# Two norm passes of a transformer kernel rearranged: who adds x, in what order the K tiles come, and from where the high parts are taken

## The reference, cut to what matters

```python
hx = rmsnorm(x, g_pre1) * (1.0 + sc1) + sh1            # the norm in front (pre1)
ux = hx @ w_in                                         # q, k, v, pooling, convolution, gates
yx = mixer_out(...)                                    # attention, pooling, convolution, merged @ w_out
x  = x + gt1 * rmsnorm(yx, g_post1)                    # the norm behind (post1), added to x
hx2 = rmsnorm(x, g_pre2) * (1.0 + sc2) + sh2           # pre2
x  = x + gt2 * rmsnorm(swiglu(hx2, w_ffn_in, w_ffn_out), g_post2)      # post2
```

## Time and profile before

| | before |
|---|---|
| median of three runs | 2203.57 us (2198.2 to 2205.74) |
| the profiled execution | 2197.6 us; the span of its instructions is 2195.8 us |
| PE busy | 2114.2 us, 96% of the span |
| DVE / ACT / POOL busy | 1335.3 / 799.6 / 772.2 us (61%, 36%, 35%) |
| mean granted clock of PE | 0.986 of full speed |

### The profile page before, as it was taken

The page is one execution under the profiler, slowest core; times in us unless marked ns, Lnnn a source line. Parts: engine busy times, 40 slices in busy tenths (PEclk is TensorE's granted clock), DMA queues, the critical chain, the costliest instruction groups (busy, mean ns, idle before and its releaser), DMA issues.

```text
span 2195.8 us, 27998 instructions
## 1 busy us (share of the span) xinstructions
PE 2114.2 (96%) x11316; PEld 1783.8 (81%) x11316; DVE 1335.3 (61%) x1807; ACT 799.6 (36%) x1173; POOL 772.2 (35%) x360
## 2 busy tenths in 40 slices
PE   8989999999999999999999989899999999999997
PEld 7777888888888888888888877778777877888885
DVE  8379899755873788757517775989854262101113
ACT  5457412234234522222212345662244343222223
POOL 3310123232335434233323345004344465444442
PEclk9999999999999999999999989999999999999998
DMA  7100011132452233533323322002222422222321
GB/s 273 58 30 1 25 58 63 48 107 92 144 193 86 74 125 122 197 104 116 107 84 114 96 75 83 26 1 82 86 93 85 141 78 96 93 91 95 96 87 67
DMA packets 63200, 202.62 MB, mean 92 GB/s; under 512 B 7136, under 2 KB 8416, under 8 KB 63072
## 3 DMA queue, kind: packets, MB, share of 16 engines
q1 hardware_dynamic: 58608, 191.56, 26.3%
q10 hardware_dynamic: 4464, 9.28, 1.2%
HBM read 195.17 MB, written 5.64 MB: 91 GB/s over the span
## 4 chain that ended last, share of the span: by engine, by line
PE 78%; DVE 18%; ACT 2%; issue 1%; DMA 0%; POOL 0%; ACTq 0%; DVEq 0%; POOLq 0%
PE ps L545 73%; DVE conv_acc L1719 3%; DVE unit_stats L1680 2%; DVE ps L1719 2%; DVE probs L1694 1%; DVE pt1l L1700 1%; DVE pt0l L1700 1%; PE ps L677 1%; PE ps L571 1%; PE ps L804 1%; DVE ada_raw L1550 1%; PE ps L647 1%; PE ps L825 1%; PE ps L656 1%; DVE acc L1441 1%
## 5 line engine op out<-in xcount | busy, mean ns | idle before, releaser
L445 POOL TENSOR_TENSOR w_l<-w_raw,w_h 128x1024 fp32r<-128x1024 f32 (+3 forms) x296 | 673.8, 2281 | 1285.5 <-ACT w_h L961 1285.2
L545 PE MATMUL ps<-h_h,w_h 128*128 128x512 f32 (+1 forms) x1296 | 428.6, 371 | 9.2 <-ACT t L1241 4.2
L545 PE MATMUL ps<-h_h,w_l 128*128 128x512 f32 (+1 forms) x1296 | 425.1, 368 | 0.0
L545 PE MATMUL ps<-h_l,w_h 128*128 128x512 f32 (+1 forms) x1296 | 425.1, 368 | 0.0
L961 ACT ACTIVATE w_h<-w_raw 128x1024 fp32r<-128x1024 f32 (+3 forms) x296 | 277.2, 938 | 222.3 <-PE ps L545 148.6
L545 PEld LDWEIGHTS ps<-h_h,w_h 128*128 128x128 f32 x1296 | 244.2, 189 | 59.3 <-ACT t L1241 6.6
L545 PEld LDWEIGHTS ps<-h_h,w_l 128*128 128x128 f32 x1296 | 244.9, 189 | 43.3
L545 PEld LDWEIGHTS ps<-h_l,w_h 128*128 128x128 f32 x1296 | 244.5, 189 | 42.4 <-issue 1.2
L1550 DVE CUSTOM_DVE_ANT_0 ps<-ada_raw,c_row 128x1024 f32<-128x1024 f32 x160 | 272.3, 1702 | 9.0 <-DMA ada_raw<-in_ada 4.0
L545 PE MATMUL ps<-f_h,w_h 128*128 128x258 f32 (+1 forms) x672 | 173.1, 339 | 0.9 <-DVE t L1905 0.9
L545 PE MATMUL ps<-f_h,w_l 128*128 128x258 f32 (+1 forms) x672 | 173.5, 340 | 0.0
(11 more groups left out here) (266 smaller groups left out, 3189.1 us busy)
## 6 DMA issues: line engine op xcount, KB each, us to landing
w_raw<-in_w SPq DMA_DIRECT2D x216, 512.0 KB, 3.6
ada_raw<-in_ada SPq DMA_DIRECT2D x80, 512.0 KB, 3.6
w_raw<-in_w SPq DMA_DIRECT2D x56, 256.0 KB, 3.0
w_raw<-in_w SPq DMA_DIRECT2D x16, 384.0 KB, 3.0
ada_near<-in_ada SPq DMA_DIRECT2D x10, 512.0 KB, 10.0
ada_far<-in_ada SPq DMA_DIRECT2D x6, 512.0 KB, 14.8
x_again<-in_x ACTq DMA_DIRECT2D x8, 384.0 KB, 7.3
x_between<-x SPq DMA_DIRECT2D x8, 384.0 KB, 2.3
```

Of the source, the lines that this page charges most:

```text
L445: nc.gpsimd.tensor_tensor(wl[:, s % RING, 0:n], raw[:, s % RAW, 0:n], wh[:, s % RING, 0:n], ALU.subtract).then_inc(split, 1)
L545: ins = nc.tensor.matmul(at(out, c0, c1), w[:, s % RING, b * P:(b + 1) * P], m[:, kt, first + c0:first + c1], start=(kt == 0 and n == 0), ...
```

## The change

Four things change.

1. The order of work at the norms between the layers and the last one. K tiles are taken in the order 0, 4, 1, 5, 2, 6, 3, 7 (`K_ORDER[1]`), by DVE, ACT, POOL and the pair on PE alike. POOL adds tiles 4 to 7 to x, one behind the other and ahead of all its subtractions; DVE multiplies those four tiles early and adds tiles 0 to 3 itself. After post2 these DVE products go to PSUM in two parts, of 512 and 256 columns (`residual_in_parts`), so that no addition of DVE reads both operands from SBUF. The room for them is a bank that the context part of the values gives up in layer 1; the copy of the values is now in layer 1 as it was in layer 0, and the bank for q0 is free once the latent half is copied.
2. High parts come straight from the scaled tile: ACT writes `h_h` (or `f_h`) with the same scale and bias as the full tile, high part first, instead of writing the tile and copying it.
3. Running sums after the feed-forward stage: at each tile DVE now adds the y squares of that tile at once, and of tile 6 all three sums, ahead of its work on tile 7.
4. PE: half of the `token_sums` comes earlier, with three matmuls of `keep_warm` between the halves, and there are more of these matmuls altogether.

`first_pair` goes; `gemm_pair` does its work from lists of PSUM pieces.

```diff
+K_ORDER = ((0, 1, 2, 3, 4, 5, 6, 7), (0, 4, 1, 5, 2, 6, 3, 7))
...
+        def key_value_pieces():
+            return ([(at(A[1], 0, CTX), 0, CTX, True, False), (at(A[1], CTX, T), CTX, T, True, True)],
+                    [(psf[:, 1024:1024 + CTX], 0, CTX, False, True), (at(A[0], CTX, T), CTX, T, True, True)])
+        def product_pieces():
+            return ((CTX, T, psf[:, 0:LAT]), (0, CTX, psf[:, 2048 + T:2048 + T + CTX]))
...
-        pool_last, pool_adds = (0, 2, 4, 6), (4, 6)
+        pool_last, pool_adds = (0, 2, 4, 6), (4, 5, 6, 7)
...                                                    (POOL)
                     pool.wait_ge(*seen("hh", ly, st, k))
-                    if (ly, st) == (0, "pre1"):
-                        pool.wait_ge(*seen("t", ly, st, k))
+                    pool.wait_ge(*seen("tb", ly, st, k))
                     nc.gpsimd.tensor_tensor(hl[:, k, lo:T], scaled_tile(k)[:, lo:T], hh[:, k, lo:T],
-                    if (ly, st) == (1, "pre1") and k in (0, 2):
-                        add_x(0, "post2", 0, pool_adds[k // 2])
...
-                    lows(1, "pre2", lo)
+                    for k in pool_adds:
+                        add_x(1, "post1", lo, k)
+                    lows(1, "pre2", lo, K_ORDER[1])
...
-                    lows(1, "pre1", 0)
+                    for k in pool_adds:
+                        add_x(0, "post2", 0, k)
+                    lows(1, "pre1", 0, K_ORDER[1])
...                                                    (PE, renorm)
                 token_sums(t3, lo, st, stop=False)
+                if nxt:
+                    take(0, "warm", ly, st)
+                    keep_warm(s, fill[0])
                 pe.wait_ge(*seen("ysq", ly, st, KT - 1))
                 token_sums(t2, lo, st, start=False).then_inc(*pe_done.up("stat", ly, st))
...
-                renorm(ly, "post1", lo, (ly, "pre2"), s0 + S_FF, (4, 8 if ly == 0 else 4))
+                renorm(ly, "post1", lo, (ly, "pre2"), s0 + S_FF, (3, 3, 8 if ly == 0 else 6))
                 if ly:
                     spread(lo, "pre2", ly, "pre2", w="OD", to=factor(ly, "pre2"))
+                    keep_warm(s0 + S_FF, 6)
...
-                renorm(ly, "post2", lo, (1, "pre1") if ly == 0 else None, SLABS, (4, 4))
+                renorm(ly, "post2", lo, (1, "pre1") if ly == 0 else None, SLABS, (3, 3, 6))
                 if ly == 0:
                     spread(0, "pre1", 1, "pre1", w="OD", to=factor(0, "pre1"))
+                    keep_warm(SLABS, 8)
...                                                    (ACT, h_high; ff_high alike)
-                for k in range(KT):
+                for k in K_ORDER[1]:
                     act.wait_ge(*seen("t", ly, st, k))
                     t = scaled_tile(k)
-                    for c0, c1, s in chunks(lo):
-                        nc.scalar.activation(t[:, c0:c1], t[:, c0:c1], ACT.Identity,
-                                             bias=mod[:, ly, shift + k, s:s + 1]).then_inc(*act_tmp.up())
-                    act.wait_ge(*act_tmp.ago())
-                    nc.scalar.activation(hh[:, k, lo:T], t[:, lo:T], ACT.Copy).then_inc(*act_hi.up("hh", ly, st, k))
+                    for out, tally, name in ((hh[:, k], act_hi, "hh"), (t, act_tmp, "tb")):
+                        for c0, c1, s in chunks(lo):
+                            ins = nc.scalar.activation(out[:, c0:c1], t[:, c0:c1], ACT.Identity,
+                                                       bias=mod[:, ly, shift + k, s:s + 1])
+                        ins.then_inc(*tally.up(name, ly, st, k))
+                        act.wait_ge(*tally.ago())
...                                                    (DVE, renorm)
+            def residual_in_parts(k):
+                for c0, c1, out in product_pieces():
+                    v.tensor_tensor(out, acc[:, k, c0:c1], factor(0, "post2")[:, c0:c1], ALU.mult).then_inc(*dve_tmp.up())
+                for n, (c0, c1, out) in enumerate(product_pieces()):
+                    dve.wait_ge(*dve_tmp.ago(1))
+                    ins = v.tensor_tensor(x[:, k, c0:c1], x[:, k, c0:c1], out, ALU.add)
+                    ins.then_inc(*dve_tmp.up(*(("x", 0, "post2", k) if n else ())))
...
                 residual(0)
-                residual(1)
+                post_scale(ly, st, lo, 4)
                 next_variance(ly, st, lo, nxt)
-                residual(2)
+                for k in pool_adds[1:]:
+                    post_scale(ly, st, lo, k)
                 dve.wait_ge(*seen("spread", *nxt))
-                for k in range(KT):
+                for k in K_ORDER[1]:
+                    if k in (1, 2, 3):
+                        residual(k)
                     scaled(k)
-                    if k + 3 < KT:
-                        residual(k + 3)
...                                                    (DVE, last feed-forward group)
-                        elif j:
-                            y_add(ly, "post2", lo, j - 1)
-                            if ly == 0:
-                                gain_adds(ly, "post2", lo, j - 1)
+                            continue
+                        if ly == 0 and 0 < j < KT - 1:
+                            gain_adds(ly, "post2", lo, j - 1)
+                        if j < KT - 1:
+                            y_add(ly, "post2", lo, j)
+                        if ly == 0 and j == KT - 2:
+                            gain_adds(ly, "post2", lo, j)
```

More of the change, by code:

```diff
@@ L549, in gemm, with gemm_pair @@
                     ins.then_inc(used, 1)
-            def gemm_pair(outs, slabs, xs, high_ready, low_ready, cols, first=0, between=None):
-                blocks = [(sa, sb, b, nb) for sa, sb, nb in slabs for b in range(nb)]
+            def gemm_pair(pieces, blocks, xs, high_ready, low_ready, first=0, between=None, after=None):
                 (xh, xl), n_k = xs, len(blocks)
                 steps = []
-                for k in range(n_k):
-                    steps += [("high", k)] + ([("low", k - 1)] if k else [])
+                for i in range(n_k):
+                    steps += [("high", i)] + ([("low", i - 1)] if i else [])
                 steps.append(("low", n_k - 1))
-                for i, (kind, k) in enumerate(steps):
-                    sa, sb, b, nb = blocks[k]
+                for n_step, (kind, i) in enumerate(steps):
+                    sa, sb, b, k = blocks[i]
                     if kind == "high":
-                        if b == 0:
+                        if i == 0 or blocks[i - 1][0] != sa:
                             pe.wait_ge(split, sb + 1)
@@ L1960, in put, with put_tiles @@
     def put(s, w, cols, k0=0, k1=KT):
[L1961 to L1962 removed]
+        put_tiles(s, w, cols, range(k0, k1))
+    def put_tiles(s, w, cols, tiles):
+        for n, k in enumerate(tiles):
+            out[s, :, n * P:(n + 1) * P] = w[k * P:(k + 1) * P, cols:cols + P]
     for n, c in ((S_KV, q_end), (S_KV + 1, q_end + KV * HD)):
[L1966 to L1967 removed]
+        put_tiles(n, w_in, c, K_ORDER[l][0:4])
+        put_tiles(n + 2, w_in, c, K_ORDER[l][4:8])
     for j in range(BR):
```

126 lines of the change are left out of this document (47 added, 79 removed).

## The result

The changed kernel takes 2190.11 us in the median of four runs (2187.24 to 2191.78) against 2203.73 before, a ratio of 0.9937 with a 95% interval of 0.9922 to 0.9951: 13.6 us faster, where 15.7 were forecast (2187.9). Its profiled execution took 2191.78 us, with a span of 2190.0.

A forecast was written before the change was run, and what follows sets the result against it. Matmuls on PE bound nearly everywhere, so edits pay only where PE waits or runs at lower clock. Terms 1.35 + 3.0 + 0.5 + 7.8 + 2.0 + 1.0 = 15.7 us took 2203.57 to 2187.9; range 2179 to 2200.

The forecast's parts named there:

- Values of layer 0: At q0 of layer 0: PE waits for one copy instead of two and keeps its clock, 1.35 and 3.0 us.
- The 1.35 of waiting: Layer 0's q0 starts near 61.7 instead of 63.05, PE's idle falling from 2.15 to 0.8: 1.35 us.
- the clock's 3.0: Behind the shorter idle at layer 0's q0, 6 us at half clock return to full: 3.0 us, other end 0.
- First norm: Layer 0's first norm: `f_h` 0.85 sooner, statistics about half a microsecond later, then ACT paces: 0.5 us, bounds -1 and +2.
- Norm between the layers: First scaled tile 4.45 us earlier, then ACT paces eight tiles at 2.3; q0 of layer 1 starts 7.8 us earlier.
- Last norm: Last norm's tiles paced by ACT at 1.5 us instead of 1.8 each: 2.0 us, or 0.4 at low clock.
- End of layer 1: Sums at the end of layer 1 half done ahead, as tile 6 is in early: 1.0 us.
- High parts: Two ACT activations from the scaled tile instead of shift and copy: loss of 0.3 us per tile where ACT paces.
- Unread matmuls: In the three norms, 52 instead of 28 matmuls whose results go unread, 20 for 8 between the layers: cost nothing.
- the second: Rival: POOL's additions block VectorE between the layers and in the last norm; 12 of 15.7 lost, 2199.9 us; chance 0.12.
- The rule of the Trainium skill weighed in the prediction: GpSimd and VectorE share an SBUF read port, so moving additions to POOL may not help; by it alone, 2199.9 us.
- The third: Rival: matmul pairs between the layers and in the last norm stay at 1.2 GHz, slower, 2213.5 us; chance 0.08.

The follow-up runs named there:

- e0: The changed kernel a second time with no edit: 2190.22 us, 0.9937 of the kernel before.
- e2: Changed kernel with the running sums in the older order, tile 6's behind the addition of tile 7, in both layers: 2196.29 us.
- e7: Changed kernel with POOL's first addition waiting for the small statistics, between the layers and in the last norm: 2189.89 us.
- e1: Changed kernel with q0 of layer 0 waiting again for both copies of the values: 2192.83 us.
- e3: Changed kernel with ACT shifting the tile, then copying it into the high part, between the layers and in the last norm: 2183.28 us.
- e6: Changed kernel with the first norm's statistics for the next norm behind DVE's last addition instead of its third: 2190.88 us.
- e8: Changed kernel with the unread matmuls as before the change, 28 instead of 52: 2188.29 us.
- e11: Changed kernel with six unread matmuls instead of three ahead of the first spread between the layers: 2191.35 us.
- e4: Changed kernel with DVE's products between the layers going back into SBUF, POOL still adding four tiles: 2188.37 us.
- e5: Changed kernel with POOL adding no tile between the layers and in the last norm, DVE adding all eight through PSUM: 2195.61 us.

## Why the prediction was right

- **Values of layer 0**, 4.35 forecast. The 1.35 of waiting came to within 0.02 (0.78 idle for 2.15). Of the clock's 3.0 the first profile shows 1.2, and so do seven others with this idle; four show 2.8. I had chosen between two values of which both occur, and the one I took is the rarer.
- **First norm**, 0.5 forecast, 0.08 measured. The step's picture was wrong, though the term was small. I let the fourth tile reach PE 1.5 us sooner and ACT set the pace from there. In the changed kernel's first profile PE had no wait there at all, being behind with matmuls at half clock; in the ten others with the hole it waits 1.3 to 1.6 us for that tile, and in e0, at the same B, it comes 19.0 us behind ACT's square of the last y, against 19.1 before. The 0.85 by which `f_h` comes sooner were lost to DVE: its first product comes 0.5 later, as foretold, and its statistics took 0.3 more (1.81 for the 1.56 of the earlier trace rows). From that tile on PE is busy all the time, so PE paces (e0_again):

```profile
732.60 0.63 PE L586 MATMUL ps<-f_h,w_h 128*128 128x258 f32 x2 [1.31 <-ACT f_h L1012]
...
732.60:744.60 12.00, 12.00 (x72) 10.72 (x73) 6.52 (x7) 11.97 (x23) 8.62 (x5) 1.00 0.09 35
```

  In the three profiles with B 33.1 the term is -1.2.
- **Norm between the layers**, 7.8 forecast, 7.72 measured: 4.40 up to the first scaled tile (4.45) and 3.32 behind it (3.35). The parts: the wait for the sum went (e2), the stretched statistics took back over 1 us (e7), ACT paces with 2.32 a tile (2.3), and q0 waits for POOL. Two errors cancelled in the first half. The first product came 0.9 later than worked out: DVE's last sum was stretched to 1.91 beside POOL, and the spread, which I had taken as warm (1.2), took 2.41 and ended only 0.1 us ahead of that sum. But from there to the first scaled tile it took 8.0 instead of the 8.8 between the two times I gave (my terms for it add up to 8.55, so the working was also 0.3 out of step with itself): tile 0 and the three products are shorter. The 4.40 is also a lucky profile: over the five with these instructions unchanged (changed, e0, e1, e3, e6) C is 21.1 to 23.7 and 22.15 in the middle, a gain of 3.35 on the one profile of before. So 7.8 against 7.72 is in part luck.
- **Last norm**, 2.0 forecast, 2.5 measured: ACT paces as foretold, and the first scaled tile came no later.
- **End of layer 1**, 1.0 forecast, 0.36 measured, in G. The sums are 0.9 earlier, but the spread behind them then takes 2.05 instead of 1.51, at the lower clock. In e7, e8 and e11, where the clock falls later, G is 6.15 to 6.26, a gain of 0.9 to 1.0: the term came out whole there.
- **High parts**: the price of 0.3 a tile was right: 2.4 in D for eight tiles (e3).
- **Unread matmuls**: at nothing, as costed (e8).

Sum 13.3 by stretches and 13.6 by medians against 15.7: most of what is missing lies in the two terms in which the clock has a say, the values of layer 0 (1.75) and the end (0.64). One part of the change stands untested: no run undoes the order of the tiles alone.

On the rivals: the second is out (e4, e5). The Trainium skill (SBUF — State Buffer, Who interferes with whom) says that a VectorE instruction with two inputs in SBUF contends with a GpSimd instruction that reads SBUF, and one with at most one such input does not, outside its two-port modes. This case agrees: 1504 ns for the additions against 947 for the products, and 1.34 against 0.17 us for a 128x6 instruction when POOL waits (e7). The rule of the Trainium skill weighed in the prediction (Perfetto Trace Analysis, Optimizing Scalar/DVE Operations), that moving work between the two might not help, did not come true here: moving four additions gained 5 us in D (e5), and D stayed as short where two of DVE's own additions were stretched (e4). The third, a pair at half clock, did not come: from 1309 us on the clock is 1.00. PE's waits there are fewer than the rival supposed, 1.17 and 0.58 in front of the second and third tile and none over 0.15 at the high parts of the others; but in e5, where it waits 0.6 to 1.35 at every tile, the clock is 1.00 too:

```profile
1310.00:1330.00 20.00, 15.19 (x77) 11.60 (x76) 14.43 (x30) 15.02 (x26) 12.79 (x8) 1.00 0.30 120
```

## What to carry to other kernels

Look for a wait of PE on work that is queued behind something later than it needs: an order of three running sums was worth nearly half of this change, and its cost showed as one row. Before a reordering, name the engine that paces behind it, and count what it does per tile: ACT's second activation took back 3 us that a copy keeps. And an edit worth 1 to 3 us is read from stretches between fixed instructions, since single times of one kernel lie 4 us apart; and of those stretches only profiles at the same clock are compared, or a gain like that of e6 may be missed.

## What the hardware showed that I had not expected

- PE's clock stood at 0.50 for 8 us while PE was busy for 4.00 of every 4.00 us (e0_again, 1294 to 1302), with one-column sums, 128-column spreads and unread matmuls. It had fallen just ahead of a wait of PE of 0.56 us, and three more wide matmuls in place of that wait did not keep it up (e11).
- The same 0.78 us of idle left the clock at 1.00 in some profiles and at half in others (A 9.5 and 11.0), and 2.15 us left it at half in both profiles that have it.
- A 128x6 instruction of DVE can take as long as POOL's subtraction of a whole tile beside it: 1.81 instead of 0.17 us.
